# One Trainium2 core, hybrid attention and mLSTM step: half of the cached keys turned by VectorE, gates in two passes

## The reference

```
aq, ak, av, mq, mk, mv, mi, mf, mo = split_in(xn  w_in)          # mi, mf: the gates, 4 columns each
aq = rms_norm(aq.reshape(B, T, H_ATT, 2, DQK_ATT), q_norm_g)      # mean of squares over 128, per head
ak = rms_norm(ak.reshape(B, T, H_ATT, 2, DQK_ATT), k_norm_g)
k_all = concatenate([cache_k[l], k_new], axis=1)                  # cache_k: 8 streams x 256 keys x (4 heads x 2 x 128)
s = einsum('bqhcd,bkhcd->bchqk', q, k) * 128 ** -0.5              # contracts the 128 of DQK_ATT
w = softmax(s)[:, 0] - lam * softmax(s)[:, 1];  o = einsum('bhqk,bkhd->bqhd', w, v)
```

## Time and profile before

| | |
|---|---|
| median of 3 runs | 1798.72 us (1798.43 to 1798.89) |
| profiled execution | 1800.59 us, span of its instructions 1798.8 us |
| TensorE busy | 1789.2 us (99%), 9718 matmuls |
| VectorE busy | 878.7 us (49%) |
| ScalarE busy | 680.9 us (38%) |
| DMA | 251.42 MB, 140 GB/s mean |

### The profile page before, as it was taken

One profiled execution on the slowest core, in us unless ns is written; L12 is line 12 of the kernel. 1 busy time (PEld: TensorE's weight loads), 2 busy tenths in 40 slices (PEclk: granted clock), 3 DMA queues, 4 the chain that ended last, 5 costly groups with the idle time before them and its releaser, 6 DMA issues.

```text
span 1798.8 us, 27842 instructions
## 1 busy us (share of the span) xinstructions
PE 1789.2 (99%) x9718; PEld 1620.6 (90%) x9718; DVE 878.7 (49%) x1683; ACT 680.9 (38%) x1296; POOL 137.3 (8%) x182
## 2 busy tenths in 40 slices
PE   9999999999999999999999999999999999999999
PEld 7999999899998888999888999888999888999887
DVE  4533675455567655554433554433544333545333
ACT  5323544444445444433323333332333323333322
POOL 3300001000111100011000111000111000111000
PEclk9999999999999999999999999999999999999999
DMA  7564346665656543444334444334444334444442
GB/s 195 169 175 123 94 111 207 190 189 148 190 175 213 154 138 118 117 128 125 122 127 128 122 123 128 123 124 128 127 119 127 128 121 124 128 120 125 146 144 97
DMA packets 297427, 251.42 MB, mean 140 GB/s; under 512 B 9341, under 2 KB 244157, under 8 KB 297357
## 3 DMA queue, kind: packets, MB, share of 16 engines
q1 hardware_dynamic: 281590, 209.76, 40.1%
q0 software_dynamic: 11088, 37.18, 6.3%
q10 hardware_dynamic: 4678, 3.53, 0.7%
HBM read 234.87 MB, written 15.56 MB: 139 GB/s over the span
## 4 chain that ended last, share of the span: by engine, by line
PE 96%; DMA 1%; DVE 1%; ACT 1%; issue 0%; ACTq 0%; POOL 0%; DVEq 0%
PE acc L502 17%; PE acc L504 17%; PE acc L503 17%; PE bank L588 8%; PE bank L589 8%; PE bank L587 8%; PE bank L1739 3%; PE ssb L587 2%; PE ssb L588 2%; PE ssb L589 2%; PE bank L1746 1%; PE ssb L1739 1%; PE bank L548 1%; PE bank L547 1%; PE bank L549 1%; PE acc L547 1%
## 5 line engine op out<-in xcount | busy, mean ns | idle before, releaser
L482 DVE TENSOR_TENSOR w_lo<-raw,w_hi 128x512 fp32r<-128x512 f32 x768 | 558.9, 735 | 840.2 <-ACT w_hi L473 839.5
L473 ACT ACTIVATE w_hi<-raw 128x512 fp32r<-128x512 f32 x768 | 483.7, 631 | 882.5 <-PE acc L504 448.8
L502 PE MATMUL acc<-x2g_hi,w_hi 128*128 128x384 f32 x1024 | 346.9, 339 | 0.0
L504 PE MATMUL acc<-x2g_hi,w_lo 128*128 128x384 f32 x1024 | 346.1, 338 | 0.0
L503 PE MATMUL acc<-x2g_lo,w_hi 128*128 128x384 f32 x1024 | 345.7, 338 | 0.0
L502 PE MATMUL acc<-a_hi,w_hi 128*128 128x400 f32 (+1 forms) x768 | 271.4, 353 | 0.2 <-DVE w_lo L482 0.2
L503 PE MATMUL acc<-a_lo,w_hi 128*128 128x400 f32 (+1 forms) x768 | 262.9, 342 | 0.0
L504 PE MATMUL acc<-a_hi,w_lo 128*128 128x400 f32 (+1 forms) x768 | 262.4, 342 | 0.0
L588 PE MATMUL bank<-w_lo,a_hi 128*128 128x512 f32 x640 | 252.9, 395 | 0.0
L589 PE MATMUL bank<-w_hi,a_lo 128*128 128x512 f32 x640 | 252.5, 395 | 0.0
L587 PE MATMUL bank<-w_hi,a_hi 128*128 128x512 f32 x640 | 252.0, 394 | 0.0
(11 more groups left out here) (332 smaller groups left out, 1527.0 us busy)
## 6 DMA issues: line engine op xcount, KB each, us to landing
raw<-in_w_up SPq DMA_DIRECT2D x128, 512.0 KB, 4.1
raw<-in_w_down SPq DMA_DIRECT2D x128, 512.0 KB, 3.8
raw<-in_w_in SPq DMA_DIRECT2D x94, 512.0 KB, 4.0
raw<-in_w_out SPq DMA_DIRECT2D x32, 512.0 KB, 3.9
kc<-in_cache_k POOLq DMA_DIRECT2D x8, 1024.0 KB, 6.4
vc<-in_cache_v POOLq DMA_DIRECT2D x8, 1024.0 KB, 9.1
C_rows<-in_state_C POOLq DMA_DIRECT2D x8, 512.0 KB, 7.5
out<-C_rows POOLq DMA_DIRECT2D x8, 512.0 KB, 5.0
```

The costliest lines, as they stand in the source:

```text
L473: e.activation(w_hi[:, q], raw[:, slot, 4 * (q % 2):4 * (q % 2) + 4, :], ACT.Copy).then_inc(hi_ready, 1)
L482: e.tensor_tensor(w_lo[:, q], raw[:, slot, 4 * (q % 2):4 * (q % 2) + 4, :], w_hi[:, q].bitcast(F32), ALU.subtract).then_inc(lo_ready, 1)
L502: e.matmul(out, w_hi[:, q, kk], hi[:, k, at], start=k == 0, stop=False, skip_group_check=True)
L504: last = e.matmul(out, w_lo[:, q, kk], hi[:, k, at], start=False, stop=k == KT - 1, skip_group_check=True)
```

## The change

It has six parts.

1. Of each stream's eight column groups of cached keys, TensorE turns four (8 squares, in one gap, slot 8b + 2, banks 0 and 1), and ScalarE copies both banks. The other four are turned by VectorE, 32 by 32, from kc straight into kT: 16 instructions per stream of 32 partitions by 256 elements, four in each of the slots 8b - 1, 8b, 8b + 1 and 8b + 2. TensorE's scores of the stream wait for them (`blocks_turned`), and so does GpSimd's next load of kc.
2. The gates' product: the remainders of the gate weights are packed beside the rounded ones in one stationary matrix (columns 32 to 39), so that two passes of 16 matmuls do for three; VectorE adds the two halves. The weights are prepared earlier, and the spread of the row norms (`rstd`) moves from ahead of the gates into their middle.
3. The sums of squares in `qk_norm`: one fp32 pass becomes two fp32r passes (n_hi, n_lo). ScalarE makes n_hi, a tile earlier than the squares were made, and also the mean that VectorE made; VectorE makes n_lo.
4. One load of x at the start moves from SyncE's queue to ScalarE's.
5. In the output projection the turned squares of the new x are laid two to a gap.
6. Buffers are moved to make room.

```
-KEYS_AT = (-4, -2)
+KEYS_AT, BLOCKS_AT = -2, (-5, -4, -3, -2)
...
-            plan += [(s + KEYS_AT[0], "keys", (step, 0)), (s + KEYS_AT[1], "keys", (step, 1))]
+            plan += [(s + KEYS_AT, "keys", step)] + [(s + at, "key_blocks", (step, i)) for i, at in enumerate(BLOCKS_AT)]
...
 GpSimd
-                done(e, ("kT", b - 1, 3))
+                done(e, ("kT", b - 1, 1))
+                e.wait_ge(S("blocks_turned"), 4 * b)
                 dma(kc[:], cache_k[0, b].rearrange("(a p) h n -> p a (h n)", p=P), "kc_in")
...
 ScalarE
+                elif q == 2:
+                    if u:
+                        e.wait_ge(S("n_done"), u)
+                    for x in range(2):
+                        b = take(e, ("n", u, x))
+                        taken(e.activation(n_mean[:, x, cols], b[:, cols], ACT.Identity, scale=1.0 / DQ,
+                                           bias=eps_col[:, 0:1]), ("n", u, x))
...
+                        for i in range(2):
+                            k = take(e, ("kT", n, i))
+                            taken(e.activation(kT[:, 2 * i:2 * i + 2].rearrange("p c k -> p (c k)"), k[:], ACT.Copy),
+                                  ("kT", n, i))
...
 VectorE
+                    elif what == "key_blocks":
+                        b, i = n
+                        if i == 0:
+                            e.wait_ge(S("kc_in"), 16 * (b + 1))
+                            if b:
+                                done(e, ("s", b - 1, 1))
+                        for j in range(4):
+                            ins = e.transpose(kT[32 * j:32 * j + 32, 4:8].rearrange("p c (a k) -> p c a k", a=2)
+                                              [:, :, :, 32 * i:32 * i + 32],
+                                              kc[32 * i:32 * i + 32].rearrange("p a (c d) -> p c a d", d=P)
+                                              [:, 4:8, :, 32 * j:32 * j + 32])
+                        ins.then_inc(S("blocks_turned"), 1)
...
 TensorE
+            e.wait_ge(S("gw_lo_made"), 1)
+            gates = fill(e, "gates")
             for k in range(KT):
-                mm(b[:, 0:TOK], gw_hi[:, 8 * k:8 * k + P], a_hi[:, k], k == 0, False)
-                mm(b[:, 0:TOK], gw_hi[:, 8 * k:8 * k + P], a_lo[:, k], False, False)
-                last = mm(b[:, 0:TOK], gw_lo[:, 8 * k:8 * k + P], a_hi[:, k], False, k == KT - 1)
+                w = gw[:, GATE_W * k:GATE_W * k + P]
+                mm(gates[:, 0:TOK], w, a_hi[:, k], k == 0, False)
+                last = mm(gates[:, 0:TOK], w, a_lo[:, k], False, k == KT - 1)
...
-                        filled(mm(b[:, pair_cols(u)], ones[:], n_sq[:, x, pair_cols(u)], True, True), ("n", u, x))
+                        mm(b[:, cols], ones_r[:], n_hi[:, u % 2, x, cols], True, False)
+                        filled(mm(b[:, cols], ones_r[:], n_lo[:, u % 2, x, cols], False, True), ("n", u, x))
...
-                    read_out(e, *[("kT", b, i) for i in range(4)])
+                    read_out(e, *[("kT", b, i) for i in range(2)])
+                    e.wait_ge(S("blocks_turned"), 4 * b + 4)
```

More of the change, by code:

```diff
@@ L71 @@
 X_HALF = (P - META) // 2
+GATE_W, GATE_LO = 64, 32
 class Uses:
@@ L1311, in qk_norm @@
                     take_av(u - 2)
-                elif q == 1:
-                    for x in range(2):
-                        b = take(e, ("n", u, x))
-                        ins = ts(n_mean[:, x, cols], b[:, cols], 1.0 / DQ, EPS, ALU.mult, ALU.add)
-                        taken(ins, ("n", u, x))
+                elif q == 2 and u + 1 < 8:
+                    n_low(u + 1)
                 elif q == 3:
@@ L1406, in att_work @@
                         e.wait_ge(S("lam_ready"), 1)
-                    elif what == "keys":
-                        i = 2 * n[1] + 1
-                        k = take(e, ("kT", n[0], i))
-                        if n[0]:
-                            done(e, ("s", n[0] - 1, 1))
-                        taken(e.tensor_copy(kT[:, 2 * i:2 * i + 2].rearrange("p c k -> p (c k)"), k[:]),
-                              ("kT", n[0], i))
+                    elif what == "key_blocks":
[10 more added lines that the diff above has]
+                        ins.then_inc(S("blocks_turned"), 1)
                     elif what == "scores":
@@ L1776, in _ @@
             mm_tile(e, 0, 1, a_hi, a_lo, at=LIVE)
-            e.wait_ge(S("diag_made"), 1)
-            b = fill(e, "rstd")
-            for r in range(4):
-                last = mm(b[:, STARTS[r]:STARTS[r] + ROWS[r]], ones[:], diag[:, r, 0:ROWS[r]], True, True)
-            filled(last, "rstd")
             e.wait_ge(S("gw_lo_made"), 1)
-            b = fill(e, "gates")
+            gates = fill(e, "gates")
             for k in range(KT):
-                mm(b[:, 0:TOK], gw_hi[:, 8 * k:8 * k + P], a_hi[:, k], k == 0, False)
-                mm(b[:, 0:TOK], gw_hi[:, 8 * k:8 * k + P], a_lo[:, k], False, False)
-                last = mm(b[:, 0:TOK], gw_lo[:, 8 * k:8 * k + P], a_hi[:, k], False, k == KT - 1)
+                w = gw[:, GATE_W * k:GATE_W * k + P]
+                mm(gates[:, 0:TOK], w, a_hi[:, k], k == 0, False)
+                last = mm(gates[:, 0:TOK], w, a_lo[:, k], False, k == KT - 1)
+                if k == KT // 2 - 1:
+                    e.wait_ge(S("diag_made"), 1)
+                    b = fill(e, "rstd")
+                    for r in range(4):
+                        ins = mm(b[:, STARTS[r]:STARTS[r] + ROWS[r]], ones[:], diag[:, r, 0:ROWS[r]], True, True)
+                    filled(ins, "rstd")
             filled(last, "gates")
```

99 lines of the change are left out of this document (65 added, 34 removed).

## The result

The changed kernel takes 1809.73 us (median of 4 runs, 1808.69 to 1810.52) against 1798.74 for the kernel before, measured beside it. The ratio is 1.0060, with a 95% interval of 1.0047 to 1.0072: slower by some 11 us. The profiled execution took 1809.06 us.

A forecast was written before the change was run, and what follows sets the result against it. TensorE, busy 96% of the chain that ended last, was taken as the bound. Waits of 19.8 us less savings of 16.1 gave +3.7 on 1798.72, 1802.4, rounded up to 1803 us; range 1792 to 1812.

The forecast's parts named there:

- rival 1: TensorE's clock falls in the two long waits, streams 0 and 1: +2 to +3 us, 1805 to 1809; chance 0.22.
- Gates with `diag`: Gates on TensorE: 16 of 48 passes go, 2.9 us, and the wait for `diag` ahead of them, 0.75 us.
- Sums of squares: Norms' gaps on TensorE: four fp32r passes at 0.73 us instead of 1.34, 0.6 a gap, 4.8 us for eight.
- Keys: Attention stage: TensorE turns one lot of 8 squares less per stream, 8 x 0.87 = 7.0 us saved.
- e1's theory A: For e1: all loss lies in the attention stage; 1787.9 us within 0.8, no TensorE wait above 1 us there.
- The price of a transpose: One VectorE transpose: 0.42 us taken; bounds 0.30, half a 512-element copy, and 0.84, twice a two-input operation.
- factor of 48: Transposes ahead of TensorE's waits, 16 for stream 0, 8 for stream 1, 4 each other: 0.1 us each is 4.8.
- rival 3: VectorE transposes near their lower bound, 0.30 to 0.36 us: 2.9 to 5.8 us less, 1796.6 to 1799.5; chance 0.15.
- The waits: Attention stage: TensorE waits for VectorE's squares at stream 0, ScalarE's kT copy at streams 1 to 7; 19.8 us.
- stream 1's keys: TensorE's wait for these keys goes, since it needs them two slots later: 0.63 us saved.
- The moved load: Load of x at the start: same bytes, same pace, before the same matmuls; costed at nothing, 0.5 us either way.
- Rival 2: Attention stage without TensorE waits, 1782.6 us; chance 0.15, including waits at only a few of eight places, up to 1795.

The follow-up runs named there:

- e3: Changed kernel with TensorE's lot of eight key squares two slots earlier, at slot 8b instead of 8b + 2; 1793.99 us, ratio 0.9972.
- e7: Changed kernel with each VectorE transpose cut into two of 128 elements, the halves following each other; 1812.99 us, ratio 1.0076.
- e1: Changed kernel with its keys part undone, TensorE turning all sixteen squares of every stream in two lots; 1790.27 us, ratio 0.9949.
- e12: e7 with its halved transposes reordered so each writes another group of 32 partitions than the last; 1823.85 us, ratio 1.0132.
- e2: Changed kernel with each lot's squares reordered to write one group of 32 partitions and read four; 1808.42 us, ratio 1.0050.
- e6: e3 plus 36 thrown-away matmuls keeping TensorE busy just before its wait at stream 0's scores; 1794.80 us, ratio 0.9972.
- e4: Changed kernel with stream 0's keys wholly turned by TensorE in two lots, as in the kernel before; 1802.02 us, ratio 1.0018.
- e8: Changed kernel with the one moved load of x back in SyncE's queue; 1808.81 us, ratio 1.0051.
- e9: e5 with GpSimd issuing the load of stream 1's keys before it waits for and stores the v columns; 1785.70 us, ratio 0.9924.
- e10: e9 with VectorE's four lots of a stream in pairs, in slots 8b - 1 and 8b + 2; 1788.89 us, ratio 0.9942.
- e5: Changed kernel with the edits of e3 and e4 together; 1788.33 us, ratio 0.9938.

## Why the prediction was right, and what was off

The forecast was 1803, with 1792 to 1812 as its range, and slower as the likeliest sign. It came out at 1809.7. What it said of places and causes holds, but its sum gave +3.7 where +11.0 came, a third. That the time lies inside the range is owed to a range that was drawn wide enough for rival 1, whose own 1805 to 1809 end just below it.

**TensorE's savings.** Gates with `diag`: 3.65 predicted, 3.95 measured (tile 1 to tile 2). Sums of squares: 4.8 predicted, 4.85 measured (tile 16 to 24). Keys: 0.87 per stream, seen in e3 stream by stream. All right. The profiled execution of before started late (14.66, against 12.81 to 13.80 in all others but e7's); of the 10.9 us at tile 24, 1.56 were there at the first matmul already. Against the medians that part doesn't count. Counted from its own first matmul, e1 is 8.5 us ahead at tile 48 (9.71 - 1.17), its median is 8.5 better, and 3.65 + 4.8 is 8.45. The last agreement is in part luck: 9.3 were won up to tile 24, and some 0.8 lost behind it, 0.6 of them in tile 24. That the late start is all that e1's theory A had wrong is argued, not shown.

**The price of a transpose.** 0.42 taken, 0.448 measured from start to start, which by the prediction's own factor of 48 is 1.3 us; the copy's half (0.30) was out by half as much again. The reason given was that an instruction which writes another group waits. By e7 and e12 that wait is real: 0.125 us for each change of group, measured at 128 elements. Less that, a square of 256 elements would stand near 0.32 (estimated from 0.448 - 0.125), inside rival 3's 0.30 to 0.36. The Trainium skill's "VectorE: DVE Perf Modes", section "Two Vector instructions with no wait between them", from which the prediction took this rule, agrees with e7 and e12. The section also holds an instruction that reads from another group, by which e2 had to come out as it did; e2 is the only run here that bears on it. In this kernel the price can't be had back by the order of whole squares, since each goes from one group to another, and two that follow each other differ in at least one of the two; e7's cut, which does bring the same groups twice, made a lot longer (2.02 against 1.78).

**The waits.** Predicted and measured, in us:

| stream | 0 | 1 | 2 | 3 | 4 | 5 | 6 | 7 | sum |
|---|---|---|---|---|---|---|---|---|---|
| predicted | 6.0 | 6.0 | 2.6 | 2.2 | 0.95 | 0.55 | 0.95 | 0.55 | 19.8 |
| measured | 7.1 | 4.0 | 2.7 | 2.4 | 1.0 | 1.0 | 1.1 | 0.9 | 20.2 |

The places, the releasers and the sum are right; that the sum agrees to 0.4 us is partly luck, since stream 1's is 2 us short and the others together longer. The trace says why. In the prediction's times (the changed kernel's plus 10.86, the lead at tile 24) ScalarE's second copy of stream 1 ends at 300.3 instead of 298.8, 1.5 us later, since VectorE ended stream 0 later by 0.9 and the load of kc took 9.8 instead of 9.3. TensorE, though, was there at 296.4 instead of 292.8, 3.6 us later, after a wait longer by 1.1 and the half clock. That is what rival 1 had ("swallowed by stream 1's"). It is read from the trace; no run takes the half clock alone out of the changed kernel, for e6 stands on e3, where this wait is gone. That the placing of the lot was the cause of the seven is shown by e3, and that stream 0's was VectorE's work by e4.

**The step that failed** was to leave the clock out of the sum. Rival 1 (0.22) is what happened, and in one more place than it said: 2.9 us behind stream 0's wait (tile 25's 9.96 less 7.09), about 1.5 behind stream 1's and 1.7 behind stream 2's (estimated as half of the 2.95 and 3.4 us that TensorE works at the half clock), 6.1 in all, part of which stream 1's shorter wait gave back. I took the two waits of 6 us to be the only dangerous ones; after 2.7 us at stream 2 it fell as well. With it the sum of the stage comes close: 20.2 + 6.1 - 7.0 (lots) - 0.6 (stream 1's keys) = 18.7, against 19.3 measured, where the prediction had 12.2. The prediction named the Trainium skill's "TensorE: Matmul & The Clock Gate", section "Why this matters for your kernels", for this; the trace agrees for the three longest waits. But stream 3's wait of 2.4 us left the clock up in the changed kernel and not in e4, stream 2's left it up in e2 and e4 at 2.7 us and in e7 at 3.2, and in e6 it fell at stream 1, where no wait is over 1.1 us and where it stayed up in e3. So no run here gives a length from which it falls, and where page and traces differ, the traces decide.

**The rest.** The moved load: costed at nothing, 0.5 either way; between tiles 0 and 1 it shows 0.6 in e8's trace, and nothing in its time. The moved mean cost 1.1 us of VectorE's time in the prediction; the 0.6 us that TensorE loses in tile 24 of e1 may come from it, but it wasn't tried alone. The x2 pairs weren't tried alone. Rival 2 (no waits, 1782.6) was ruled out with the argument that ScalarE's second copy comes behind one that was just in time. That holds for the slot that the change chose. e3 shows that two slots earlier it costs nothing, and with stream 0 left to TensorE and stream 1's keys loaded first the kernel comes to 1785.7 (e9).

**Left open.** e9 gives back 1.2 us in tiles 27, 29 and 31 (0.55, 0.43 and 0.26) that later streams don't; e10 tried one cause and was worse. Why the clock fell at stream 1 in e6 and not in e3 is open. The 0.6 us of the stage's loss that the sum leaves over have no cause yet. What a shorter lot would be worth wasn't measured, only what a longer one costs.

## What to carry to other kernels

Work taken off the bounding engine is worth its price only if what takes its place is done in time, and that is decided by the slot, not by the share of busy time: here VectorE was at 49% and ScalarE at 38%, and the same work cost 19.5 us in one placing, 3.7 in another (e3 against e1) and, with stream 0 left to TensorE, brought some 5 in a third (e9 against e1: 4.6 by the times, 5.4 by the differences to the times of before beside each). Ask of every copy out of a PSUM bank what needs that bank next, and leave slots in between; of every load, what its queue waits for first; and hand over nothing at the start of a stage, where the helper comes in late. A wait of some us on TensorE can also cost clock behind it (here 2.9 us behind a wait of 7.1, and an estimated 1.5 and 1.7 behind waits of 4.0 and 2.7), so count that too. A wait close behind may swallow part of it.

## What the runs showed of the hardware

- A STREAM_TRANSPOSE of 32 partitions by 256 fp32 elements takes 0.448 us from start to start in a row, and one of 128 elements 0.315, when each writes another group of 32 partitions than the last (for 256 elements it is the same where the group that is read changes, e2). Half the size is far from half the price: an estimated 1.04 ns an element and 0.18 us fixed (from 0.448 - 0.315 over 128), most of the latter being the 0.125 of the next point.
- With the same groups as the last one, the instruction behind it comes 0.125 us sooner (e7 against e12).
- A longer lot costs more than its length: 0.49 us more per lot (e12 against e7) cost 10.9 us, 22 times as much, by longer waits (30.6 us in sum against 23.1) and five falls of the clock instead of three.
- A load of 1 MB of keys took 9.6 us from issue to landing right behind GpSimd's three stores of v (e5), and 7.3 when it was issued before them (e9).
- The first real matmul started between 12.81 and 15.97 us in the profiled executions of these kernels, with all but one of the loads in front alike. One execution's start is no evidence for or against an edit there.
